# Five matmuls per weight block instead of six: the high and low activations of 250 tokens side by side in one matmul

## The reference

```
x += W_out[ concat(diff-attention 512 | mLSTM 256 | short conv 256) ]( RMSNorm(x) @ w_in )
x += CrossAttention_4heads( RMSNorm(x) @ w_cq, memory @ w_ck, memory @ w_cv ) @ w_co
x += ( silu(RMSNorm(x) @ w_gate) * (RMSNorm(x) @ w_up) ) @ w_down        # 1024 -> 2816 -> 1024
```

## Time and profile before

| | |
|---|---|
| Time, median of three runs | 1917.35 us (1912.59 to 1920.39) |
| Span of the profiled execution, first to last instruction | 1913.9 us |
| Busy share of the span: PE / weight loads / DVE / ACT | 96% / 91% / 51% / 31% |
| Mean granted clock of PE | 0.984 |

### The profile page before, as it was taken

How to read it: one execution, slowest core, us unless ns; L and a number is a source line. 1 busy time by engine, 2 the same in 40 slices (tenths; PEclk the granted TensorE clock), 3 DMA queues, 4 the chain that set the end, 5 groups by cost and what they waited for, 6 DMA issues and landing times. The chain is left out here.

```text
span 1913.9 us, 35113 instructions
## 1 busy us (share of the span) xinstructions
PE 1833.7 (96%) x14681; PEld 1743.8 (91%) x14681; DVE 967.8 (51%) x2170; ACT 589.2 (31%) x1051; POOL 2.2 (0%) x7
## 2 busy tenths in 40 slices
PE   6998999999999999999989899999999999999997
PEld 5988888998899999999979788899988999999996
DVE  4565667544454434434545637765444443343345
ACT  4221345323332212212322114443234222222233
POOL 0000000000000000000000000000000000000000
PEclk9999999999999999999989989999999999999998
DMA  5313323322323233332232332242241233233222
GB/s 161 85 51 54 79 71 112 116 76 84 98 73 96 89 89 89 89 88 84 73 85 67 50 66 73 81 142 78 77 128 56 79 89 98 78 89 98 79 83 86
DMA packets 303475, 164.64 MB, mean 86 GB/s; under 512 B 16121, under 2 KB 299721, under 8 KB 303309
## 3 DMA queue, kind: packets, MB, share of 16 engines
q1 hardware_dynamic: 303308, 162.29, 30.1%
HBM read 151.07 MB, written 11.16 MB: 85 GB/s over the span
## 5 line engine op out<-in xcount | busy, mean ns | idle before, releaser
L911 PE MATMUL proj<-xg_hi,w_hi 128*128 128x272 f32 x1664 | 446.2, 287 | 0.0
L910 PE MATMUL proj<-xg_lo,w_hi 128*128 128x272 f32 x1664 | 445.9, 287 | 0.0
L1350 DVE TENSOR_TENSOR w_lo<-raw,w_hi 128x1024 fp32r<-128x1024 f32 (+1 forms) x268 | 323.0, 1205 | 125.8 <-ACT w_hi L1165 125.0
L910 PE MATMUL proj<-xn_lo,w_hi 128*128 128x272 f32 x1376 | 375.5, 291 | 0.0
L911 PE MATMUL proj<-xn_hi,w_hi 128*128 128x272 f32 x1376 | 374.5, 291 | 0.0
L908 PE MATMUL proj<-xg_hi,w_lo 128*128 128x272 f32 x1664 | 346.6, 290 | 0.0
L1165 ACT ACTIVATE w_hi<-raw 128x1024 fp32r<-128x1024 f32 (+1 forms) x268 | 276.7, 1037 | 176.3 <-PE proj L911 171.9
L908 PE MATMUL proj<-xn_hi,w_lo 128*128 128x272 f32 x1376 | 298.4, 299 | 19.0 <-DVE w_lo L1345 16.4
L910 PEld LDWEIGHTS proj<-xg_lo,w_hi 128*128 128x128 f32 x1664 | 313.1, 188 | 0.0
L911 PEld LDWEIGHTS proj<-xg_hi,w_hi 128*128 128x128 f32 x1664 | 313.0, 188 | 0.0
L910 PEld LDWEIGHTS proj<-xn_lo,w_hi 128*128 128x128 f32 x1376 | 263.9, 192 | 0.0
(11 more groups left out here) (320 smaller groups left out, 1974.7 us busy)
## 6 DMA issues: line engine op xcount, KB each, us to landing
raw<-in_w_in SPq DMA_DIRECT2D x54, 512.0 KB, 3.7
raw<-in_w_gate SPq DMA_DIRECT2D x44, 512.0 KB, 3.8
raw<-in_w_up SPq DMA_DIRECT2D x44, 512.0 KB, 3.8
raw<-in_w_down SPq DMA_DIRECT2D x32, 512.0 KB, 3.6
raw<-in_w_ck SPq DMA_DIRECT2D x16, 512.0 KB, 3.6
raw<-in_w_cv SPq DMA_DIRECT2D x16, 512.0 KB, 3.5
raw<-in_w_out SPq DMA_DIRECT2D x16, 512.0 KB, 3.6
raw<-in_w_cq SPq DMA_DIRECT2D x16, 512.0 KB, 3.5
```

The costliest lines, as they stand in the source:

```text
L910: mm(pb[h][:, 0:HALF], wh, xl[:, a:b], start=False, stop=False)
L911: last = mm(pb[h][:, 0:HALF], wh, xh[:, a:b], start=False, stop=final)
L1350: v.tensor_tensor(w_lo[:, s, 0:nt, :], raw[:, r, 0:nt, :], w_hi[:, s, 0:nt, :].bitcast(F32), ALU.subtract).then_inc(split_lo, 1)
```

## The change

The 544 tokens are no longer cut at 272 but at `GA = 250`; the rest is `GB = 294`. High and low activations now lie in one tensor (`xn`, `xg`, `hid_hl`, `[128, 2, 8, 544]`), so one matmul can take the high and the low part of the first 250 tokens as 2 x 250 = 500 columns, with the output in one bank: `high x w_hi` in columns 0 to 249, `low x w_hi` in columns 250 to 499. The other 294 tokens are multiplied as before. The `w_lo` product of the first 250 tokens is added to the second half of the bank.

```diff
-                                for h, (a, b) in enumerate(HALVES):
-                                    mm(pb[h][:, 0:HALF], wl, xh[:, a:b], start=first, stop=False)
-                                for h, (a, b) in enumerate(HALVES):
-                                    mm(pb[h][:, 0:HALF], wh, xl[:, a:b], start=False, stop=False)
-                                    last = mm(pb[h][:, 0:HALF], wh, xh[:, a:b], start=False, stop=final)
+                                both = pb[0][:, 0:2 * GA].rearrange("p (n t) -> p n t", n=2)
+                                mm(both, wh, x2[:, :, 0:GA], start=first, stop=False)
+                                mm(pb[1][:, 0:GB], wh, xl[:, GA:T], start=first, stop=False)
+                                mm(pb[1][:, 0:GB], wh, xh[:, GA:T], start=False, stop=False)
+                                mm(pb[0][:, GA:2 * GA], wl, xh[:, 0:GA], start=False, stop=final)
+                                last = mm(pb[1][:, 0:GB], wl, xh[:, GA:T], start=False, stop=final)
```

```diff
+PAIRED = ("gates", "ml", "o", "b", "c", "h", "qa", "ka", "va", "cq", "gate", "up")
...
+                        if kind in PAIRED:
+                            act.wait_ge(unit_done, n + 1)
+                            af(pair[:, u["slot"], :], proj[u["slot"]][0][:, GA:2 * GA], ACT.Copy).then_inc(pair_in, 1)
...
-                            for h, (a, b) in enumerate(HALVES):
-                                src = proj[s][h][rows, 0:HALF]
...
+                            joined = join(dst[:, 0:GA], rows)
+                            times(GA, T, proj[s][1][rows, 0:GB]).then_inc(slot_free[s], 1)
+                            dve.wait_ge(own_dve, joined)
+                            return times(0, GA, dst[:, 0:GA]).then_inc(slot_free[s], 1)
+
+                        def join(dst, rows=slice(0, P)):
+
+                            own[0] += 1
+                            v.tensor_tensor(dst, pair[rows, s, :], proj[s][0][rows, 0:GA], ALU.add).then_inc(own_dve, 1)
+                            return own[0]
 
                         dve.wait_ge(unit_done, n + 1)
+                        if kind in PAIRED:
+                            dve.wait_ge(pair_in, PLAN.pairs[kind, j])
...
-                            for h, (a, b) in enumerate(HALVES):
-                                v.tensor_tensor(xT[:, j, a:b], xT[:, j, a:b], proj[s][h][:, 0:HALF], ALU.add).then_inc(slot_free[s], 1)
+                            own[0] += 1
+                            v.tensor_tensor(xT[:, j, 0:GA], xT[:, j, 0:GA], proj[s][0][:, GA:2 * GA], ALU.add).then_inc(own_dve, 1)
+                            v.tensor_tensor(xT[:, j, GA:T], xT[:, j, GA:T], proj[s][1][:, 0:GB], ALU.add).then_inc(slot_free[s], 1)
+                            dve.wait_ge(own_dve, own[0])
+                            v.tensor_tensor(xT[:, j, 0:GA], xT[:, j, 0:GA], proj[s][0][:, 0:GA], ALU.add).then_inc(slot_free[s], 1)
```

More of the change, by code:

```diff
@@ L292, in __init__ @@
         self.slot_freed, freed = [], [0, 0]
-        for n, (kind, _, _) in enumerate(self.tiles):
+        self.pairs = {}
+        for n, (kind, j, _) in enumerate(self.tiles):
             freed[n % 2] += 1 if kind == "ck" else 2
             self.slot_freed.append(freed[n % 2])
+            if kind in PAIRED:
+                self.pairs[kind, j] = len(self.pairs) + 1
         self.fills, self.filled_before = {}, {}
@@ L356, in hybrid_streaming_encoder_step @@
         const = sb("const", [P, C_HOT])
-        ones = sb("ones", [P, P])
+        ones = sb("ones", [P, L_M])
+        pair = sb("pair", [P, 2, GA])
         sq = sb("sq", [P, 2, T])
@@ L1359, in scaled, with times @@
                         def scaled(dst, by=1.0, rows=slice(0, P)):
-                            for h, (a, b) in enumerate(HALVES):
-                                src = proj[s][h][rows, 0:HALF]
+                            def times(a, b, src):
                                 if by == 1.0:
[L1364 to L1368, removed]
@@ L1369, in scaled @@
-                            return last
+                                    return v.tensor_tensor(dst[:, a:b], src, rstd[rows, a:b], ALU.mult)
+                                return v.scalar_tensor_tensor(out=dst[:, a:b], in0=src, scalar=by, in1=rstd[rows, a:b],
+                                                              op0=ALU.mult, op1=ALU.mult)
+                            joined = join(dst[:, 0:GA], rows)
+                            times(GA, T, proj[s][1][rows, 0:GB]).then_inc(slot_free[s], 1)
@@ L1372, in evacuate @@
                         if kind == "gates":
-                            for h, (a, b) in enumerate(HALVES):
-                                v.tensor_tensor(gst[:, 0, a:b], proj[s][h][0:H_M, 0:HALF], rstd[0:H_M, a:b], ALU.mult)
-                                v.tensor_tensor(gst[:, 1, a:b], proj[s][h][32:32 + H_M, 0:HALF], rstd[32:32 + H_M, a:b],
-                                                ALU.mult).then_inc(slot_free[s], 1)
+                            join(gst[:, 0, 0:GA], slice(0, H_M))
@@ new lines, in evacuate @@
+                            joined = join(gst[:, 1, 0:GA], slice(32, 32 + H_M))
+                            v.tensor_tensor(gst[:, 0, GA:T], proj[s][1][0:H_M, 0:GB], rstd[0:H_M, GA:T], ALU.mult)
+                            v.tensor_tensor(gst[:, 1, GA:T], proj[s][1][32:32 + H_M, 0:GB], rstd[32:32 + H_M, GA:T],
+                                            ALU.mult).then_inc(slot_free[s], 1)
+                            dve.wait_ge(own_dve, joined)
+                            v.tensor_tensor(gst[:, 0, 0:GA], gst[:, 0, 0:GA], rstd[0:H_M, 0:GA], ALU.mult)
@@ L1406, in evacuate @@
                             v.tensor_copy(ubuf[:, SEQ + 2:SEQ + 4], u_st[:, j, :])
[L1407 to L1410, removed]
+                            joined = join(ubuf[:, 2:2 + GA])
+                            k = SEQ - GA
+                            v.tensor_tensor(ubuf[:, 2 + GA:2 + SEQ], cbuf[:, GA:SEQ], proj[s][1][:, 0:k], ALU.mult)
+                            v.tensor_tensor(ubuf[:, 4 + SEQ:4 + T], cbuf[:, SEQ:T], proj[s][1][:, k:GB], ALU.mult).then_inc(slot_free[s], 1)
+                            dve.wait_ge(own_dve, joined)
+                            v.tensor_tensor(ubuf[:, 2:2 + GA], ubuf[:, 2:2 + GA], cbuf[:, 0:GA], ALU.mult).then_inc(slot_free[s], 1)
                             tile_read(dve, "h", j)
```

57 lines of the change are left out of this document (32 added, 25 removed).

## The result

The changed kernel takes 1952.05 us (median of four runs, 1948.94 to 1956.19) beside 1918.82 for the kernel before (four runs here, the three listed above and one more). The ratio is 1.0179, 95% interval 1.0146 to 1.0212: slower by 1.8%, 33 us, where 1890 us and a gain of 1.5% were forecast. The profiled execution has a span of 1948.6 us, 34.7 more than before.

A forecast was written before the change was run, and what follows sets the result against it. PE was taken to bound the kernel, its projection blocks filling 73% of the span. 38 us less from matmuls and 12 more from exposed waits gave -26 on 1913.9, so 1888, about 1890 as median; range 1868 to 1928.

The forecast's parts named there:

- Step (1): PE's projection blocks: 500-wide matmul 213 ns, 294-wide 133, 250-wide 118; block 730 ns against 750.3, 38 us less.
- proportional to columns: Rival on PE's matmuls: cost follows columns, block stays at 750 ns, only evacuations' 12 us remain: 1929 us; chance 0.13.
- Step (3): Places where PE already waits (scores, `vh`, weight splits, L564 sums): waits grow, 12 us in all, bounds 4 and 25.
- Step (2): Evacuations in steady stages: up to 0.75 us later but covered; the tightest, the `up` tile, keeps 0.41 us spare.
- the evacuation becomes the bound at every tile: Rival: copy and join delay `up` tiles by over 1.16 us, PE waits at all 44: about 1950 us; chance 0.05.
- the slow form of a matmul under 256 columns: Rival: the 250-wide matmul leaves the fast form, 418 ns each, costing 560 us: 2470 us; chance 0.02.
- The estimate made from it: Skill's formula on PE's blocks: 695 to 692.5 ns, an estimated 5 us gained before any cost.

The follow-up runs named there:

- cut250: Kernel before, six matmuls a block and old evacuation, cut at token 250 instead of 272: 1939.77 us, ratio 1.0118 to before.
- onestretch: Changed kernel, its 500-wide matmul reading 500 neighbouring high-activation columns, low part of the first 250 tokens left out: 1942.14 us, ratio 1.0119 to before.
- evac256: Kernel before with six matmuls cut at 256, plus the change's layout and evacuation with zeros as added terms: 1936.30 us, ratio 1.0116 to before.
- bf16dense: Kernel before with all six matmuls in bf16 and one dense constant table as moving operand, activations left out: 1809.45 us, one run.
- cut256: Kernel before, six matmuls a block and evacuation in two instructions, cut at token 256 instead of 272: 1916.98 us, ratio 1.0016 to before.
- fused256: Changed kernel with the cut at 256 instead of 250 (512, 3 x 288, 256 columns a block): 1939.22 us, ratio 1.0105 to before.
- bf16cross: Kernel before with the two cross products in bf16, reading the upper two bytes of each word; high x high stays fp32r: 1947.94 us, ratio 1.0168.
- lo16: Kernel before with low activations stored as dense bf16 and the high weights x low activations product in bf16: 1902.58 us, ratio 0.9952.
- bf16all: Kernel before with all six matmuls of a block in bf16, reading the upper two bytes of each four-byte word: 1873.28 us, one run.

## Why the prediction was wrong

**Step (1), the 500-wide matmul, failed.** The prediction took 213 ns, by the plain f32 pass of 256 columns that hides its weight load. That rested on the reading that the surplus *is* the weight load. The wide matmuls show that it isn't: with one load each, 500 columns have a surplus of 19 ns and 512 one of 18 to 20, where 272 have 11 to 12, and with a load less at 256 the block doesn't move. The plain pass takes 215 ns for 256 columns, a word every two cycles of 2.4 GHz, so it says nothing of a stream with one a cycle. The rows that spoke for this were there: 120 / 256 = 0.469 and 125.2 / 272 = 0.460 were in the rival "proportional to columns", given 0.13; 227 / 500 = 0.454 is in line with them. The surplus grows with the width. The 38 us of gain were 0. Against the forecast's 730 ns a block of `xg` takes 757: of the 27 ns the 500-wide matmul brings 17 (230 in the mean), the three 294-wide ones 13 (135 to 138 where 133 were forecast), and the 250-wide one takes 4 back.

**The cut at column 250 was named and not priced.** The start of the second read stood in that rival as a thing that might bring it about. cut250 shows the cut to be worth 4 to 10 ns a block of six matmuls. In the change the blocks are (688 x 5.4 + 832 x 9.5 - 352 x 1.3) ns = 11 us longer than before. The jump between the two stretches, the other thing that the rival named, can bear these 11 us as well: onestretch has the same cut without the jump, and its blocks are 8.3, 9.6 and 1.7 ns shorter than the change's, 14 us in all. How the two share the loss isn't known.

**Step (3), the exposed places, was mis-sized: 12 us, and evac256 has 19.** PE's waits grew by 10.0 us where 12 were forecast, but that they come so near is luck: two of the places named didn't grow, and 5.3 us come from one that wasn't named. evac256's price of 19 us is also more than its waits show, 5 us in all. The direction was right, and `vh`, `qc` and the norm sums grew by what was said: 0.8 each for the first two, 0.3 for the last. The largest term was on no list. L1096 waits for `att_o`, which DVE scales behind the evacuation of a `va` tile. Timeline of ACT, DVE and PE of the changed kernel, where that happens:

```profile
262.32 0.71 ACT L1279 ACTIVATE s_a<-s_a,s_neg 128x512 f32<-128x512 f32 x1
...
263.02 0.36 ACT L1192 ACTIVATE pair<-proj 128x250 f32<-128x250 f32 x1
...
263.47 0.41 DVE L1389 TENSOR_TENSOR vh<-pair,proj 128x250 f32<-128x250 f32 x1 [1.91 <-ACT pair L1192]
...
264.50 0.90 DVE L1715 SCALAR_TENSOR_TENSOR att_o<-att_o,par,work 128x32 f32<-128x32 f32 x2
...
265.45 0.79 PE L1096 MATMUL work<-aT,vtok_a 128*128 128x128 f32 x2 [2.33 <-DVE att_o L1715]
```

and the same place before:

```profile
257.42 0.79 DVE L1364 TENSOR_TENSOR vh<-proj,rstd 128x272 f32<-128x272 f32 x2
...
258.13 1.09 DVE L1681 SCALAR_TENSOR_TENSOR att_o<-att_o,par,work 128x32 f32<-128x32 f32 x2
...
258.24 0.71 ACT L1265 ACTIVATE s_a<-s_a,s_neg 128x512 f32<-128x512 f32 x1
...
259.27 0.71 PE L1086 MATMUL work<-aT,vtok_a 128*128 128x128 f32 x4 [0.22 <-DVE att_o L1681]
```

Before, DVE evacuated `vh` from 257.42, without regard to ACT, which was at the exponentials of the attention step at that time (the second begins at 258.24), and PE waited 0.22 us. After, ACT's copy of the tile stands behind those exponentials in ACT's queue; it starts at 263.02, right after them. DVE can't begin until 263.47, the scale of `att_o` behind it ends at 265.40, and PE, which had been done with its matmuls at 263.1, waits 2.33 us. The prediction named ACT's queue for what stands behind the copy; the cost was in what stands ahead of it. It added 0.75 us a place, the lengths of the copy and of the third DVE instruction, where here the wait grew by 2.1 us, nearly three times that.

**The clock was left out.** A stretch with such a wait, from the windows of the changed kernel (columns: us, busy of PE, PEld, DVE, ACT, POOL, granted clock, DMA share, GB/s):

```profile
260.00:270.00 10.00, 7.67 (x48) 6.86 (x47) 7.00 (x21) 4.52 (x12) 0.00 (x0) 0.83 0.01 2
```

and the same place before:

```profile
252.00:262.00 10.00, 9.78 (x76) 8.38 (x76) 8.78 (x35) 3.94 (x10) 0.00 (x0) 1.00 0.18 53
```

Before, PE was busy for 9.78 of 10 us and the clock at 1.00; after, it was busy 7.67, and the granted clock fell to 0.83 in the mean: from 265.3 to 268.7, straight behind the wait of 2.33 us, it reads 0.50, the lower level of 1.2 GHz. As PE is busy there, these 3.4 us at half speed cost an estimated 1.7 us beside the wait itself. In the whole profile PE's clock is at the lower level for 79.0 us, before for 60.1. Over the changed kernel's four runs the mean clock is 0.978, over seven runs of before 0.983: 0.005 of 1950 us is 10 us. 11 from the blocks, 10 from PE's waits and 10 from the clock make 31 of the 33 us. The three aren't wholly apart, since the lower clock follows waits, and cut250 has a clock of 0.977 with no more waiting than before; that part has no cause here.

**Step (2) held.** The third instruction and the copy are hidden in the steady stages. Timeline around an `up` tile after, the weight split and the matmul that needs it:

```profile
601.35 1.23 DVE L1364 TENSOR_TENSOR w_lo<-raw,w_hi 128x1024 fp32r<-128x1024 f32 x1 [0.22 <-ACT w_hi L1175]
...
603.17 0.40 PE L917 MATMUL proj<-xg,w_hi 128*128 128x500 f32 x1
```

The split ends at 602.58 and PE starts at 603.17: 0.59 us spare, where 0.41 were forecast with a shorter unit and 0.57 without. The rival that the evacuation becomes the bound at every tile is refuted, and so is the slow form of a matmul under 256 columns: 114 ns at 250. That the first of these had 1950 us, nearest of all to the 1952 measured, is chance. The rival whose mechanism came nearest, cost proportional to columns, had 1929; it lacks the 11 us of the blocks and 7 of the evacuations' 19, and it too left out the clock.

The Trainium skill, "TensorE: Matmul & The Clock Gate", section "Back-to-back issue gap", gives N / 2.4 + 2.5 ns for an isolated warm matmul, by which 272 columns come to an estimated 115.8 ns. The bf16dense stream agrees with 115.9, the fp32r stream with 124.5 to 125.6 doesn't. The estimate made from it, that the change brings next to nothing on PE, was nearer than the forecast.

## What to carry to other kernels

Merging matmuls saves only what a matmul costs beside its columns. Before counting on it, divide the distance between starts by the columns at two widths that lie far apart (256 and 272, the only ones in the trace of before, couldn't settle it): if the quotient barely moves, as from 250 to 512 here, fewer and wider matmuls bring next to nothing. And when one engine's queue takes over a piece of another's work, look at what stands ahead of it there at the places where the bound engine already waits, not at how long the piece takes.

## What the runs showed of the hardware that was not expected

- fp32r matmuls follow each other at 0.45 to 0.48 ns a column from 250 to 512 columns (114, 120, 125, 135 to 140, 227, 231 to 233 ns at 250, 256, 272, 294, 500, 512), and dense bf16 ones at 0.426 (115.9 ns at 272). At the lower level of the clock the fp32r surplus is gone: 1360 ns a block of 1632 columns, before and in cut256, evac256 and fused256.
- bf16 read with a step of four bytes takes 121 to 122 ns at 272 columns, between the two.
- Cutting the moving operand at byte 1000 of its row makes a block of six matmuls 4 to 13 ns longer than cutting at byte 1024 (cut250 against cut256: 4.4, 3.8 and 12.6 ns on xn, xg and hid). At the lower level of the clock it is 20 ns, and the same 20 for a cut at byte 992.
- Changing the type of a matmul's operands from one to the next costs some 8 ns each time (worked out from the blocks of bf16cross and lo16).
- The first fp32r matmul behind other work took 207 ns or more to the next start instead of 125, in 102 places before; a bf16 one there took 115 to 129 (lo16) or 121 to 135 (bf16all).
